# w_in as an upper and a lower half on both operands with x stationary, all of it in the first four jobs, and w_out in the last four

## What is computed

```python
h = rms_norm(x, g_mix)
(aq, ak, av, bq, bk, bv, ccq, cckv, ckr, dq, dk, dv, dfl) = jnp.split(h @ w_in, offs, axis=-1)
# oa: window attention, ob: differential attention, oc: latent attention, od: forgetting attention
x = x + jnp.concatenate([oa, ob, oc, od], axis=-1) @ w_out
x = x + jnp.square(jax.nn.relu(rms_norm(x, g_mlp) @ w_up)) @ w_down
x = x + (ple.astype(x.dtype) @ w_ple) * jax.nn.sigmoid(rms_norm(x, g_ple) @ w_ple_gate)
```

## Time and profile before

| what | value |
| --- | --- |
| median of three runs | 3703.09 us |
| the profiled execution, span | 3704.1 us |
| TensorE busy | 3558.6 us, 96% |
| layer 0, from x ready to the last job's end | 30 to 746.4 us |
| layer 1, the same | 1861 to 2575 us |
| mean granted TensorE clock | 0.977 |

### The profile page before, as it was taken

One profiled execution on the slowest core, in us unless ns is written; L12 is line 12 of the kernel. 1 busy time (PEld: TensorE's weight loads), 2 busy tenths in 40 slices (PEclk: granted clock), 3 DMA queues, 4 the chain that ended last, 5 costly groups with the idle time before them and its releaser, 6 DMA issues.

```text
span 3704.1 us, 55831 instructions
## 1 busy us (share of the span) xinstructions
PE 3558.6 (96%) x19972; PEld 2988.3 (81%) x19972; DVE 1360.8 (37%) x2203; ACT 984.7 (27%) x1462; POOL 1540.4 (42%) x734
## 2 busy tenths in 40 slices
PE   8999999989999999999999999998999999999988
PEld 4456547689999999999954564576999999999988
DVE  3234533375033150425332344334730422304263
ACT  1112221232332333322311122212333333333322
POOL 1000000066666666667520000001666666666664
PEclk9999999999999999999999999998999999999999
DMA  5323213244444444444342222232444444444433
GB/s 127 89 81 94 74 56 106 69 130 152 149 138 152 143 148 150 141 149 141 117 102 86 86 81 70 67 102 84 135 150 143 148 148 142 149 140 150 150 120 120
DMA packets 262876, 442.48 MB, mean 119 GB/s; under 512 B 15408, under 2 KB 78544, under 8 KB 262000
## 3 DMA queue, kind: packets, MB, share of 16 engines
q1 hardware_dynamic: 255456, 420.40, 36.7%
q0 software_dynamic: 7184, 18.64, 2.0%
HBM read 430.30 MB, written 8.82 MB: 119 GB/s over the span
## 4 chain that ended last, share of the span: by engine, by line
PE 90%; DVE 6%; issue 3%; ACT 1%; DMA 0%; DVEq 0%; POOL 0%; SPq 0%; ACTq 0%; POOLq 0%
PE ps L610 18%; PE ps L612 18%; PE ps L611 18%; PE ps L668 17%; PE ps L691 6%; PE ps L703 4%; PE ps L772 2%; DVE xhi L1168 1%; PE ps L807 1%; PE ps L776 1%; PE ps L775 1%; PE ps L741 1%; DVE xlo L1171 1%; PE ps L756 1%; PE ps L811 1%
## 5 line engine op out<-in xcount | busy, mean ns | idle before, releaser
L566 POOL TENSOR_TENSOR wlo<-ring,whi 128x1024 fp32r<-128x1024 f32 x600 | 1462.0, 2438 | 841.2 <-ACT whi L1006 841.2
L1006 ACT ACTIVATE whi<-ring 128x1024 fp32r<-128x1024 f32 x600 | 636.9, 1063 | 1450.5 <-PE ps L612 1450.5
L610 PE MATMUL ps<-xhi,wlo 128*128 128x320 f32 x2560 | 801.5, 313 | 22.7 <-issue 16.0
L612 PE MATMUL ps<-xhi,whi 128*128 128x320 f32 x2560 | 798.5, 312 | 0.0
L611 PE MATMUL ps<-xlo,whi 128*128 128x320 f32 x2560 | 793.9, 310 | 0.0
L668 PE MATMUL ps<-ring,xg 128*128 128x512 f32 (+3 forms) x2112 | 746.0, 509 | 14.1 <-ACT xg L999 10.0
L610 PE MATMUL ps<-hhi,wlo 128*128 128x320 f32 x2176 | 676.6, 311 | 21.8 <-DVE hhi L1481 16.1
L612 PE MATMUL ps<-hhi,whi 128*128 128x320 f32 x2176 | 677.3, 311 | 0.0
L611 PE MATMUL ps<-hlo,whi 128*128 128x320 f32 x2176 | 673.1, 309 | 0.0
L668 PEld LDWEIGHTS ps<-ring,xg 128*128 128x128 f32 x2112 | 402.0, 194 | 305.9 <-issue 271.3
L610 PEld LDWEIGHTS ps<-xhi,wlo 128*128 128x128 f32 x2560 | 485.5, 190 | 27.7 <-issue 25.9
(11 more groups left out here) (264 smaller groups left out, 2344.3 us busy)
## 6 DMA issues: line engine op xcount, KB each, us to landing
ring<-in_w_up SPq DMA_DIRECT2D x256, 512.0 KB, 3.7
ring<-in_w_down SPq DMA_DIRECT2D x256, 512.0 KB, 3.6
ring<-in_w_in SPq DMA_DIRECT2D x120, 512.0 KB, 3.6
ring<-in_w_out SPq DMA_DIRECT2D x64, 512.0 KB, 3.8
ring<-in_w_ple_gate SPq DMA_DIRECT2D x64, 512.0 KB, 3.6
ring<-in_w_in SPq DMA_DIRECT2D x16, 288.0 KB, 2.8
ring<-in_w_in SPq DMA_DIRECT2D x16, 264.0 KB, 2.7
ring<-in_w_ple SPq DMA_DIRECT2D x8, 512.0 KB, 3.6
```

The lines of the kernel that those rows point to most:

```text
L566: nc.gpsimd.tensor_tensor(wlo[:, s, :], ring[:, s, :], whi[:, s, :].bitcast(f32), ALU.subtract)\
L610: mm(out, lo[:, k, cols], xh, start=start, stop=False)
L612: return mm(out, hi[:, k, cols], xh, start=False, stop=stop)
L1006: A(whi[:, s, :], ring[:, s, :], ACT.Copy).then_inc(hi_ready, 1)
```

## The change

Each element of w_in and of x times gain is now split. ScalarE writes the upper half of each w_in unit into `whi` (`halves`), GpSimd the lower half in place of the unit in the ring (`rlo`, `lower_in_place`, four instructions of 256 columns to a full unit). ScalarE writes x times gain into `xw` as its upper half, VectorE subtracts for the lower halves (`first_split`): of the 256 prompt frames into `xv`, of the 64 sample frames into the columns of `xw` that were unused. A block of a piece is then three fp32r matmuls for tiles 0 and 1 and two for tile 2, where the lower half of x makes 64 further rows of the result; `copy_chunk` adds these with one more instruction. x stays the stationary operand.

All pieces of w_in stand in jobs 0 to 3, in the order B, D, C. The first round of w_out is 8 blocks deep, two parts to a block, in jobs 4 and 5; the second is 4 deep, one part to a block, in jobs 6 and 7. Places V of jobs 4 to 7 hold nothing, nor do V0 and V1 of job 0, V1 of job 2 and V0 of job 3.

To make room, B's projections lie where x lay. x is written to DRAM (`xsave`, four transfers of 640 KB) ahead of the loads of units 5 to 8 and read back at the end of job 3. All small loads and stores are on SyncE's queue, between the weight loads (`beside`). The upper halves for a unit stand in ScalarE's program three units ahead (`LEAD`), at the place in which TensorE ends a unit.

```diff
+        proj_b = sb("proj_b", [128, 3, 1536], at=at)
+        xw = sb("xw", [128, KB, XW], f32r, early)
+        xv = sb("xv", [128, KB, 256], f32r, early + 4 * KB * XW)
+        rlo = sb("rlo", [128, RING, 1024], f32r, at)
+        whi = sb("whi", [128, RING, 1024], f32r)
+        xsave = nc.dram_tensor("xsave", (128, KB, TOK), f32).ap()
...
+               "D": [(5, 8, 2, 512, 0), (6, 4, 4, 256, 1288), (7, 8, 2, 512, 512), (8, 8, 2, 264, 1024)],
+               "C": [(9, 4, 4, 256, 0), (10, 8, 2, 288, 256)]}
...
+        FILL = {0: {"prep": 7, "copied": 1, "T0": 9, "T1": 7, "T2": 10, "V2": 1, "T3": 9, "V3": 1, "out": 3},
+                1: {"prep": 3, "copied": 1, "T0": 8, "T1": 11, "V1": 1, "T2": 10, "V2": 1, "T3": 9, "V3": 1, "out": 3},
+                2: {"prep": 8, "copied": 1, "S0": 3, "T0": 12, "V0": 2, "T1": 10, "out": 8},
+                3: {"prep": 10, "copied": 1, "S0": 5, "T0": 12, "T1": 14, "V1": 2, "out": 8}}
...
+        OUT_K = [(0, 8), (8, 12)]
+        OUT_PARTS = (2, 1)
+        OUT_UNIT = (1, 2)
+        OUT_FILL = {4: {"norm": 4, "lat": 8, "T0": 1, "T1": 1, "T2": 1, "T3": 1},
+                    5: {"lat": 8, "copied": 1, "T0": 2, "T1": 2, "T2": 2, "T3": 1},
+                    6: {"norm": 4, "prep": 1, "T0": 1, "T1": 1, "T2": 1, "T3": 1},
+                    7: {"prep": 1, "T0": 2, "T1": 2, "T2": 1, "T3": 1}}
...
+        LEAD = 3
+        HALVES = {place: [POS[no, u] + LEAD for no, u, t in todo if t == 2 and POS[no, u] + LEAD < N_WU]
+                  for place, todo in AT.items()}
...
+            def beside(l, i):
+
+                if i == RING:
+                    first_loads(l)
+                for b in range(4):
+                    if i == SAVE_AT + b:
+                        sp.dma_start(xsave[:, 4 * b:4 * b + 4, :], x[:, 4 * b:4 * b + 4, :]).then_inc(x_saved, 16)
+                    if i == BACK_AT + b:
+                        if b == 0:
+                            hold(job_out, l * 8 + 5)
+                            hold(stored["B"], 16 * N_STORED["B"] * (l + 1))
+                            sp.wait_ge(x_saved, 64 * (l + 1))
+                        sp.dma_start(x[:, 4 * b:4 * b + 4, :], xsave[:, 4 * b:4 * b + 4, :]).then_inc(x_back[b], 16)
+                for g in "ABCD":
+                    if i == STORE_AT[g]:
+                        store_group(l, g)
+                for j in range(len(GROUPS)):
+                    if i == KEYS_AT[j]:
...
+                def lower_in_place(n, cols):
+
+                    s = n % RING
+                    hold(hi_ready, l * HL + n + 1)
+                    for c in range(0, cols, LO_COLS):
+                        w = min(LO_COLS, cols - c)
+                        last = nc.gpsimd.tensor_tensor(rlo[:, s, c:c + w], ring[:, s, c:c + w],
+                                                       whi[:, s, c:c + w].bitcast(f32), ALU.subtract)
+                    last.then_inc(lo_ready, 1)
+
...
+                hold(ext_ready, 4 * l + 4)
+                with pool.Fori(0, TAIL // RING) as u4:
...
+                n = POS[no, u]
+                if (u, t) == (0, 0) and no > 1:
...
+                    hold(lo_ready, l * HL + n + 1)
                     if no == 0:
-                        hold(gained, l * KB + min(KB, (u + 1) * nk + 1))
+                        hold(xsplit, l * KB + min(KB, (u + 1) * nk))
+                hi, lo = (w[:, n % RING, 0:nk * ncol].rearrange("p (a n) -> p a n", a=nk) for w in (whi, rlo))
+                out = ps[:, chunk_bank(no) + t, 0:ncol]
...
                 for k in range(nk):
                     kk = u * nk + k
-                    last = mm(out[:, 0:ncol], xg[:, kk * TOK + t * 128:kk * TOK + t * 128 + 128], wv[:, k, :],
-                              start=(kk == 0), stop=(kk == KB - 1))
+                    head = xw[:, kk, t * 128:(t + 1) * 128]
+                    mm(out, head, lo[:, k, :], start=(kk == 0), stop=False)
+                    if t < 2:
+                        mm(out, xv[:, kk, t * 128:(t + 1) * 128], hi[:, k, :], start=False, stop=False)
+                    last = mm(out, head, hi[:, k, :], start=False, stop=(kk == KB - 1))
...
+                if part == 0 and b < 3 and r == 0:
+                    hold(proj_copied, (l + 1) * N_WIN)
+                elif part == 0:
                     hold(wout_added, l * 2 * KB + r * KB + b - 2)
+                if (r, b, part) == (0, 0, 1):
+                    hold(hid_copied, l * 16 + 8)
...
+            def halves(l, units):
+
+                for n in units:
+                    s = n % RING
+                    _, _, nk, ncol, _ = CHUNK_AT[STREAM[n][0]]
+                    act.wait_ge(raw_loaded[s], 16 * (l * SLOT + n // RING + 1))
+                    act.wait_ge(unit_used, l * UNITS + n + 1)
+                    A(whi[:, s, 0:nk * ncol], ring[:, s, 0:nk * ncol], ACT.Copy).then_inc(hi_ready, 1)
...
                 gain_pass(l)
+                halves(l, range(4, 11))
                 rms_root(l, 0, ps[:, 3, 0:3], rroot[:, 0:3])
-                act.wait_ge(proj_copied, l * N_WIN + 2)
+                halves(l, range(11, N_UP + LEAD))
+                act.wait_ge(proj_copied, l * N_WIN + DONE_A)
                 norm(l, "A")
                 for j, g in enumerate(GROUPS):
...
+            def first_split(l):
+
+                dve.wait_ge(mix_loaded, 16 * (l + 1))
+                for b in range(KB):
+                    dve.wait_ge(gained, l * KB + b + 1)
+                    g, head = gains[:, 0, b:b + 1], xw[:, b, :].bitcast(f32)
+                    V.scalar_tensor_tensor(out=xv[:, b, :], in0=x[:, b, 0:256], scalar=g, in1=head[:, 0:256],
+                                           op0=ALU.mult, op1=ALU.subtract)
+                    V.scalar_tensor_tensor(out=xw[:, b, TOK:XW], in0=x[:, b, 256:TOK], scalar=g, in1=head[:, 256:TOK],
...
+                done(last)
+                V.scalar_tensor_tensor(out=dst[0:DSEQ, :], in0=src[DSEQ:128, :], scalar=rtok[0:DSEQ, 2:3], in1=dst[0:DSEQ, :],
+                                       op0=ALU.mult, op1=ALU.add).then_inc(proj_copied, 1)
...
-                squares_pass(l, 0)
+                first_split(l)
+                first_squares(l)
```

377 lines of the change are left out of this document (202 added, 175 removed), and 6 rows, old and new, of tables (FILL, WIN).

## The result

The changed kernel takes 3658.8 us (median; 3653.7 to 3666.6) where the kernel before takes 3703.0: a ratio of 0.9885, 95% interval 0.9868 to 0.9902. It is faster, by 44 us; the forecast was 65 us, and its range held the time. The sum of the prediction goes by the profiled executions: 3704.1 before, 3661.7 after, 42.4 us less where 66 were expected.

What follows compares the result with a forecast made beforehand. TensorE was taken to bound the kernel, busy for 90% of the chain. 3704.1 us - 208 (w_in's products) + 2 x (35 + 18 waits + 18 clock) = 3638 us; range 3565 to 3705 us.

Steps and rivals of the forecast that it cites:

- w_in's products: TensorE's w_in matmuls in both layers: fp32r at 0.227 us per 512 columns saves 208 us, bounds 188 to 229.
- second rival: fp32r at 512 columns costs the skill's formula, 0.011 us less per new matmul: 31 us less, 3607 us; chance 0.11.
- Idle time: TensorE's added waits per layer: 35 us in jobs 4 to 7, 18 us in A's pieces and jobs 0 to 3.
- lat: Fill in jobs 4 and 5: TensorE waits 4.6 us for VectorE's addition before w_out's block 5; 10 us for both.
- "norm" of job 6: Fill in job 6: w_out's fourth block waits for an addition behind VectorE's gains; 7.5 us idle, 2.5 more until the addition.
- the values' waits: Empty places V: the product with the values waits for copies of probabilities; 19 us in jobs 4 to 7, 5 earlier.
- the layer's start: VectorE's subtraction of two blocks comes between ScalarE's first blocks and TensorE's first matmul: 0.7 us per layer.
- Unit 4's wait: Each layer: unit 4's load stands behind some 25 small loads on SyncE's queue, so TensorE waits 4 us (0 to 8).
- The clock: TensorE falls to 1.2 GHz behind about half of the waits, some 2 us each: 18 us a layer (5 to 40).
- fourth rival: TensorE stays at 1.2 GHz for most of jobs 4 to 7: 62 us a layer more, 3762 us; chance 0.07.
- The supply of a unit: Load, ScalarE and GpSimd halves take 7.9 us against 10.9 us in hand: 3 us to spare, priced at nothing further.
- The tails: The two tail stages after the layers are not touched by the change, so no effect was expected there.

Runs made afterwards that it cites:

- e3: Changed kernel with the 23 small loads ahead of unit 4's load on SyncE's queue spread over the loads of later units; 3659.9 us.
- e1: Changed kernel with VectorE adding the first finished w_out block of fills 'lat' (jobs 4, 5) and 'norm' (job 6) inside the norm; 3615.2 us.
- e2: Changed kernel with TensorE running matmuls of constants in places V of jobs 4 to 7 and ahead of the output's transposes; 3634.7 us.
- e4: Changed kernel without the products of x's lower half of the 256 prompt frames with w_in's upper half, six matmuls a block, not eight; 3582.3 us.
- e12: e11 with further matmuls of constants in three more waits: ahead of the transposes of jobs 0 and 2 and the flog product in job 6; 3567.2 us.
- e8: Changed kernel with small loads spread, x saved ahead of units 13 to 16, and VectorE's square of x cut into 16 instructions; 3656.3 us.
- e13: e12 with GpSimd's half of a unit in one instruction of 1024 columns, not four of 256; 3596.1 us.
- e9: Changed kernel with the edits of e1, e2 and e8 together; 3602.8 us.
- e11: e9 with x squared by ScalarE, in four instructions between its halves, in place of VectorE; 3586.0 us.

## Why the prediction came out as it did

- **w_in's products, -208 us:** right, to the third digit of a matmul. Its bounds were not: 0.214 and 0.235 at 512 columns, with the other widths as they are, give 228 and 195, not 229 and 188; nothing hangs on it. The addition of 0.0134 us from the earlier trace rows holds at 512 columns too: 0.2266 is 0.0133 more than 512 / 2.4 GHz (0.2133). So the second rival falls. The Trainium skill (TensorE: Matmul & The Clock Gate, "Back-to-back issue gap") has 2.5 ns there, for an isolated matmul; for these the measurement decides.
- **Idle time, +53 us a layer:** right as a sum (54.3 and 53.7) and in its large places. "lat" 5.3 and 5.2 us in the first layer where I had 4.6 and the addition; "norm" of job 6 7.2 for 7.5; the transposes of jobs 0 and 2 2.7 and 3.8 for 3 and 4.8; the values' waits 43 us in both layers for 2 x 24; SyncE's wait at job 2's end 3.3 and 4.6 for 3. Some of this is luck. The term for the values in jobs 4 to 7 was 11 x 1.4 + 5 x 0.97, which is 20 and not 19, and rested on ScalarE's copy being late in 11 of 16 items. It came last in 4 and 2 of them; the sums, 18.0 and 16.6 us, came near because the waits for VectorE's copy took 0.97 to 1.11 us each, above the 0.89 of the earlier trace rows. At the layer's start I had 0.7 us and it is 3.4 (5.59 for 2.24 us, 11.17 for 7.78). VectorE's splits take up to 0.96 us in place of 0.47 while GpSimd works, some 1.7 us over two blocks; that is the exclusion which I had counted only for the norms, and the rest is open. Unit 4's wait was right in size in both layers. In cause it was right in the first alone; in the second it was VectorE's square, which the prediction had named beside the sum and priced at nothing. Behind the small loads the square stood next, so taking them away gained nothing (e3).
- **The clock, 18 us a layer:** this is the step that failed. It was 33 and 47 us. That the clock falls behind waits was right (e1, e2), but the price was not: about half of the waits, some 2 us each. A low stretch had a deficit of 1.7 or 3.4 us or more, and there were 28 more of them in two layers, for the 34 new waits that I had counted: 136 - 42 = 94 us of deficit, 3.4 each, of which 80 fell on matmuls where 36 were expected. In the earlier trace rows I had seen only waits around 1 us and took my price from them; the waits of 3 to 7 us, which are new, were followed by a low stretch nearly each time. The granted clock of jobs 4 to 7 is 0.89 and 0.85, under the 0.9 that I had set as a sign of being wrong. The fourth rival, which I gave 0.07, did not come true by its own terms: it decides from 33 us a layer above my count, and the clock cost 15 and 29 above it.
- **The supply of a unit, nothing:** right for this kernel (5 waits, 18.3 us, of which 9.8 at unit 4), and near its edge, as e4 showed.
- **The tails, nothing:** wrong by 21.5 us, in favour of the change.

Put together: -208 + 108 + 80 in the layers gives -20, and the tails and the start -22.6. The range held because it was made wide enough for the clock and because the tails gave 21.5 us back, not because the sum was good.

## What to carry to other kernels

When work is taken off the bounding engine, count what each remaining chain of the others is long, and let the fills be no shorter; and count behind every new wait the slow clock too, which here cost 80 us of matmul time beside 108 us of waiting. A wait that can't be removed can be filled with matmuls of constants: 20 us of useless work a layer made this kernel 23 us faster. Three more filled waits (e12) came with another 19 us, but the profile does not show that the filling did it. An addition that frees a buffer belongs into the first gap of its engine, not at the end of its chain; this one edit was worth 40 us.

## What I had not expected of the hardware

- GpSimd can be kept out for longer than one instruction of VectorE: 16 in a row held one GpSimd instruction for 7.14 us (e8). Another run of VectorE's instructions in the same execution did not, so this is no rule. A 64-column instruction of VectorE took 2.37 us beside GpSimd's of 1024 columns (e13). A reduction over one operand did not: beside VectorE's reduction of 9.2 us the GpSimd instructions of the changed kernel took 0.73 us.
- The tail's matmuls, the same instructions with the same types, run 1% faster in the changed kernel. A window of 100 us of the kernel before and one of the changed kernel, both at full clock:

```profile
2700.00:2800.00 100.00, 100.00 (x684) 100.00 (x683) 32.60 (x40) 30.82 (x29) 67.42 (x30) 1.00 0.46 148
```

```profile
2700.00:2800.00 100.00, 100.00 (x694) 100.00 (x694) 19.07 (x27) 31.27 (x30) 70.01 (x30) 1.00 0.44 152
```

By these windows that is 0.1462 us a matmul and 0.1441. Over all pairs of starts in the tails at full clock it is 0.1472 and 0.1460, which makes 17.6 us for the 14208 matmuls; TensorE's busy time there fell by 16.1 us. Another 6 are a shorter wait for the halves of the last heads, 5.28 us and 4.58 for 8.33 and 7.72. Operands lie at other places in SBUF since the change, but no run here moved them alone, so the cause stays open. In e2, e9 and e11 the two tails took 2220 to 2225 us together and not 2211 as in the other kernels whose layers are in the table, at the same 0.1460 us, which is open too.
